# Gate and up projections of a two-layer decoder: one plain step instead of two, ten of eleven steps by seven products

## The reference

```python
def swiglu(h, w_gate, w_up, w_down):
    return (jax.nn.silu(h @ w_gate) * (h @ w_up)) @ w_down

for i in range(DEPTH):                      # DEPTH = 2
    ...                                     # token mixer of layer i
    h = rmsnorm(x, g[2])
    x = x + rmsnorm(swiglu(h, ffn_w_gate[i], ffn_w_up[i], ffn_w_down[i]), g[3])
```

## Time and profile before

| | |
|---|---|
| median of three runs | 1316.03 us (1315.64 to 1317.51) |
| the profiled execution | 1315.58 us |
| its span in the trace | 1313.8 us |
| TensorE busy | 1303.6 us, 99% of the span |
| VectorE busy | 992.3 us, 76% |
| ScalarE busy | 603.2 us, 46% |
| granted TensorE clock, mean | 1.00 of full speed (2.4 GHz) |
| DMA, mean | 110 GB/s |

### The profile page before, as it was taken

One profiled execution on the slowest core, in us unless ns is written; L12 is line 12 of the kernel. 1 busy time (PEld: TensorE's weight loads), 2 busy tenths in 40 slices (PEclk: granted clock), 3 DMA queues, 4 the chain that ended last, 5 costly groups with the idle time before them and its releaser, 6 DMA issues. The chain is left out here.

```text
span 1313.8 us, 19204 instructions
## 1 busy us (share of the span) xinstructions
PE 1303.6 (99%) x7897; PEld 1158.9 (88%) x7897; DVE 992.3 (76%) x1041; ACT 603.2 (46%) x741; POOL 70.1 (5%) x113
## 2 busy tenths in 40 slices
PE   9999999999999999999999999999999999999998
PEld 5888888888889999999888999888898999998886
DVE  7997777789668788887587576577478888874893
ACT  7453444346443444444263455557345344442551
POOL 1000000000010000000000121022010000000000
PEclk9999999999999999999999999999999999999999
DMA  7262515245434333324503132314233233317001
GB/s 257 70 227 65 168 33 162 71 160 186 167 97 129 97 113 93 105 76 159 194 0 113 33 113 72 104 48 161 65 119 106 82 112 97 113 49 272 33 32 64
DMA packets 103414, 145.10 MB, mean 110 GB/s; under 512 B 3581, under 2 KB 77565, under 8 KB 102823
## 3 DMA queue, kind: packets, MB, share of 16 engines
q1 hardware_dynamic: 93168, 136.65, 31.5%
q10 hardware_dynamic: 10166, 7.32, 1.8%
HBM read 137.65 MB, written 8.41 MB: 111 GB/s over the span
## 5 line engine op out<-in xcount | busy, mean ns | idle before, releaser
L2422 PE MATMUL ps<-h_hi,w_hi 128*128 128x256 f32 (+1 forms) x688 | 224.8, 327 | 0.0
L2424 PE MATMUL ps<-h_hi,w_lo 128*128 128x256 f32 (+1 forms) x688 | 223.7, 325 | 0.0
L2423 PE MATMUL ps<-h_lo,w_hi 128*128 128x256 f32 (+1 forms) x688 | 223.6, 325 | 0.0
L1555 DVE TENSOR_TENSOR w_lo<-raw,w_hi 128x2048 fp32r<-128x2048 f32 (+2 forms) x62 | 120.9, 1952 | 72.2 <-ACT w_hi L951 43.3
L2422 PE MATMUL ps<-w_hi,act_hi 128*128 128x512 f32 x432 | 168.7, 391 | 0.1
L2424 PE MATMUL ps<-w_hi,act_lo 128*128 128x512 f32 x432 | 168.2, 389 | 0.0
L2423 PE MATMUL ps<-w_lo,act_hi 128*128 128x512 f32 x432 | 168.1, 389 | 0.0
L2422 PEld LDWEIGHTS ps<-h_hi,w_hi 128*128 128x128 f32 x688 | 130.9, 190 | 10.7
L2424 PEld LDWEIGHTS ps<-h_hi,w_lo 128*128 128x128 f32 x688 | 130.9, 190 | 10.7
L2423 PEld LDWEIGHTS ps<-h_lo,w_hi 128*128 128x128 f32 x688 | 130.9, 190 | 10.4
L1168 ACT ACTIVATE w_hi<-w_sum 128x1024 fp32r<-128x1024 f32 x48 | 50.9, 1061 | 122.0 <-DVE w_sum L1897 122.0
(11 more groups left out here) (333 smaller groups left out, 3233.4 us busy)
## 6 DMA issues: line engine op xcount, KB each, us to landing
raw<-in_ffn_w_down SPq DMA_DIRECT2D x14, 1024.0 KB, 5.7
x<-in_ret_w_in SPq DMA_DIRECT2D x13, 1024.0 KB, 5.2
raw<-in_ffn_w_up SPq DMA_DIRECT2D x24, 512.0 KB, 4.4
raw<-in_ffn_w_gate SPq DMA_DIRECT2D x24, 512.0 KB, 3.9
raw<-in_ret_w_in SPq DMA_DIRECT2D x10, 1024.0 KB, 5.3
down_raw<-in_ffn_w_down SPq DMA_DIRECT2D x8, 1024.0 KB, 10.2
raw<-in_diff_w_in SPq DMA_DIRECT2D x8, 1024.0 KB, 5.4
tmp<-in_ffn_w_gate SPq DMA_DIRECT2D x12, 512.0 KB, 3.9
```

The source lines that it names most:

```text
L1555: nc.vector.tensor_tensor(out_ap, whole, high.bitcast(F32), ALU.subtract).then_inc(done, 1)
L2422: nc.tensor.matmul(out_ap, a_hi, b_hi, start=start, stop=False, skip_group_check=shared)
L2423: nc.tensor.matmul(out_ap, a_hi, b_lo, start=False, stop=False, skip_group_check=shared)
L2424: return nc.tensor.matmul(out_ap, a_lo, b_hi, start=False, stop=stop, skip_group_check=shared)
```

## The change

PLAIN goes from 2 to 1: step 1 of each layer is now done by seven products, and the two calls of `columns`, with their two `prep` on ScalarE and VectorE and the second plain silu and hidden, go away. VectorE and ScalarE get an order of their own for the first step by seven. The sums T1 and T2 of that step are made in `boundary`, ahead of the last two `pre_low`, and its four pieces are loaded into the places (`raw`) where the two plain units were loaded. The places of all later pieces shift by two. TensorE's own code loses the two lines and is otherwise the same. Left out of the diff below: the places' semaphore counts in the down projection.

```diff
@@ -53,7 +53,7 @@
 RETO_N = RET_HEADS * RET_DV // (2 * P) - 4
 FFN_N = FT // 2
 DOWN_N = FFN_N - 4
-PLAIN = 2
+PLAIN = 1
 GU_U = [RETO_U + RETO_N, 0]
 DN_U = [GU_U[0] + 2 * PLAIN, 0]
 DIFF_U = DN_U[0] + DOWN_N
@@ -86,13 +86,14 @@
 PRODUCTS = ("B11", "T2", "T1", "T3", "B21", "B22", "T4")
 LEFT = {"B11": "A11", "T2": "S2", "T1": "S1", "T3": "S3", "B21": "A12", "B22": "S4", "T4": "A22"}
 USED = Order((n, f) for n in SEVEN for f in PRODUCTS)
-SUMS = Order((n, f) for n in SEVEN for f in ("T1", "T2", "T4", "T3"))
-HIGHS = Order([(PLAIN, f) for f in ("T4", "B21", "B22", "B11", "T2", "T1", "T3")]
+SUMS = Order([(PLAIN, f) for f in ("T1", "T2", "T3", "T4")] + [(n, f) for n in SEVEN[1:] for f in ("T1", "T2", "T4", "T3")])
+HIGHS = Order([(PLAIN, f) for f in ("B11", "T2", "T1", "T3", "B21", "B22", "T4")]
               + [(n, f) for n in SEVEN[1:] for f in ("B11", "T1", "T2", "T3", "B21", "B22", "T4")])
-LOWS = Order([(PLAIN, f) for f in ("T4", "B21", "B22", "B11", "T2", "T1", "T3")]
+LOWS = Order([(PLAIN, f) for f in ("B11", "T2", "T1", "T3", "B21", "B22", "T4")]
              + [(n, f) for n in SEVEN[1:] for f in ("B11", "T2", "T1", "T3", "B21", "B22", "T4")])
-S_SUMS = Order((0, f) for f in ("A21", "A22", "A11", "S1", "A12", "S2", "S3", "S4"))
-S_PARTS = Order((0, f) for f in ("S1", "S2", "S4", "S3"))
+S_SUMS = Order((0, f) for f in ("A21", "A22", "S1", "A11", "S2", "A12", "S4", "S3"))
+S_PARTS = Order((0, f) for f in ("S2", "S1", "S3", "S4"))
+PIECE_LOADS = (7, 7, 8, 8, 7, 7)
 
 
 DOWN = ("B11", "T1", "T2", "B21", "T3", "B22", "T4")
...
@@ -455,25 +456,25 @@
 
         def piece(l, n, f):
 
-            at = (4 * (n - PLAIN) + BLOCKS.index(f)) % 6
+            at = (4 * (n - PLAIN) + BLOCKS.index(f) + 2) % 6
             if at < 2:
                 return flat_tmp[:, at * HALF:(at + 1) * HALF]
             slot = (GU_U[l] + at // 2 - 1) % 2
             return raw[slot][:, at % 2 * HALF:(at % 2 + 1) * HALF]
 
         def piece_sem(n, f):
-            return piece_in[(4 * (n - PLAIN) + BLOCKS.index(f)) % 6]
+            return piece_in[(4 * (n - PLAIN) + BLOCKS.index(f) + 2) % 6]
 
         def piece_count(l, n, f):
-            p = 4 * (n - PLAIN) + BLOCKS.index(f)
-            return 16 * ((7 if p % 6 < 4 else 6) * l + p // 6 + 1)
+            p = 4 * (n - PLAIN) + BLOCKS.index(f) + 2
+            return 16 * (PIECE_LOADS[p % 6] * l + p // 6 + (p % 6 > 1))
 
         def form_sum(l, n, f):
 
             if f == "T4":
                 return t4_sum
             if n == PLAIN:
-                return early({"T1": 0, "T2": 1, "T3": 2}[f])
+                return early({"T1": 5, "T2": 6, "T3": 7}[f])
             slot, half = {"T2": (0, 1), "T1": (1, 0), "T3": (1, 1)}[f]
             return w_sum[(GU_U[l] + slot) % 2][:, half * HALF:(half + 1) * HALF]
 
@@ -791,11 +792,11 @@
 
             def load_piece(l, n, f):
                 p = 4 * (n - PLAIN) + BLOCKS.index(f)
-                if p < 2:
+                if p < 4:
+                    sp.wait_ge(w_split, GU_U[l] + p // 2 + 1 + PRIME)
+                elif p < 6:
                     sp.wait_ge(pre_turned, ST * (2 * l + 2))
                     sp.wait_ge(x_added, ST * (2 * l + 1))
-                elif p < 6:
-                    sp.wait_ge(w_split, GU_U[l] + p // 2 + 2 + PRIME)
                 else:
                     m, old = PLAIN + (p - 6) // 4, BLOCKS[(p - 6) % 4]
                     sp.wait_ge(t_made, SUMS.at(l, m, {"B11": "T1", "B12": "T3", "B22": "T3", "B21": "T4"}[old]))
...
@@ -1157,7 +1158,7 @@
                 if n > PLAIN:
                     act.wait_ge(form_used, USED.at(l, n - 1, f))
                 else:
-                    done = {"B11": 3, "T2": 3, "T1": 4, "T3": 4, "B21": 2, "B22": 2, "T4": 0}[f]
+                    done = {"B11": 0, "T2": 0, "T1": 1, "T3": 1, "B21": 2, "B22": 2, "T4": 0}[f]
                     act.wait_ge(w_used, GU_U[l] + done + PRIME)
                 if f[0] == "B":
                     act.wait_ge(piece_sem(n, f), piece_count(l, n, f))
@@ -1199,17 +1200,13 @@
                 nc.scalar.activation(u2, u2, ACT.Silu).then_inc(sil2_made, 1)
 
             def gate_up(l):
-                u = GU_U[l]
-                first, second = u % 2, (u + 1) % 2
-                prep(u + 2, first, used=u)
-                for f in ("S1", "S2", "S4"):
-                    left_high(l, f)
-                prep(u + 3, second, used=u + 1)
+                first = GU_U[l] % 2
+                form_high(l, PLAIN, "B11")
+                left_high(l, "S2")
+                form_high(l, PLAIN, "T2")
+                left_high(l, "S1")
+                form_high(l, PLAIN, "T1")
                 plain_silu(l, 0)
-                for f in ("T4", "B21", "B22", "B11", "T2"):
-                    form_high(l, PLAIN, f)
-                plain_silu(l, 1)
-                form_high(l, PLAIN, "T1")
                 left_high(l, "S3")
                 form_high(l, PLAIN, "T3")
                 for n in SEVEN:
@@ -1217,6 +1214,11 @@
                     if n > PLAIN:
                         second_silu(l, n - 1)
                     copy_p1(l, n)
+                    if n == PLAIN:
+                        form_high(l, n, "B21")
+                        left_high(l, "S4")
+                        form_high(l, n, "B22")
+                        form_high(l, n, "T4")
                     if more:
                         form_high(l, n + 1, "B11")
                     if n > PLAIN:
@@ -1647,6 +1649,9 @@
                 post_add(c, 3)
                 pre_scale(c + 1, 2)
                 pre_scale(c + 1, 3)
+                if c % 2 == 0:
+                    weight_sum(c // 2, PLAIN, "T1")
+                    weight_sum(c // 2, PLAIN, "T2")
                 pre_low(c + 1, 2)
                 pre_low(c + 1, 3)
 
...
@@ -1942,40 +1947,54 @@
 
             def gate_up(l):
                 u = GU_U[l]
-                prep(u + 2, u % 2)
                 dve.wait_ge(w_used, u + PRIME)
                 dve.wait_ge(h_split, ST * (2 * l + 2))
                 whole_left("A21")
                 whole_left("A22")
+                left_add(l, "S1", "A21", "A22", ALU.add)
                 whole_left("A11")
-                left_add(l, "S1", "A21", "A22", ALU.add)
+                left_add(l, "S2", "S1", "A11", ALU.subtract)
                 whole_left("A12")
-                left_add(l, "S2", "S1", "A11", ALU.subtract)
+                left_add(l, "S4", "A12", "S2", ALU.subtract)
+                form_low(l, PLAIN, "B11")
+                left_low(l, "S2")
+                form_low(l, PLAIN, "T2")
+                left_low(l, "S1")
+                form_low(l, PLAIN, "T1")
                 left_add(l, "S3", "A11", "A21", ALU.subtract)
-                left_add(l, "S4", "A12", "S2", ALU.subtract)
-                for f in ("S1", "S2", "S4"):
-                    left_low(l, f)
-                prep(u + 3, (u + 1) % 2)
-                for f in ("T1", "T2", "T4", "T3"):
-                    weight_sum(l, PLAIN, f)
-                plain_hidden(l, 0)
-                for f in ("T4", "B21", "B22", "B11", "T2", "T1"):
-                    form_low(l, PLAIN, f)
+                weight_sum(l, PLAIN, "T3")
                 left_low(l, "S3")
                 form_low(l, PLAIN, "T3")
-                plain_hidden(l, 1)
+                plain_hidden(l, 0)
                 for n in SEVEN:
                     more = n < FFN_N - 1
-                    if n > PLAIN:
-                        make_c21(l, n - 1)
+                    if n == PLAIN:
+                        make_u2(l, n)
                         form_low(l, n, "B21")
-                        second_hidden(l, n - 1)
+                        left_low(l, "S4")
+                        make_u4(l, n)
                         form_low(l, n, "B22")
+                        weight_sum(l, n, "T4")
+                        form_low(l, n, "T4")
+                        make_c22(l, n)
+                        form_low(l, n + 1, "B11")
+                        for f in ("T1", "T2", "T4"):
+                            weight_sum(l, n + 1, f)
+                        form_low(l, n + 1, "T2")
+                        form_low(l, n + 1, "T1")
+                        weight_sum(l, n + 1, "T3")
+                        make_c12(l, n)
+                        form_low(l, n + 1, "T3")
+                        first_hidden(l, n)
+                        continue
+                    make_c21(l, n - 1)
+                    form_low(l, n, "B21")
+                    second_hidden(l, n - 1)
+                    form_low(l, n, "B22")
                     if more:
                         form_low(l, n + 1, "B11")
                     make_u2(l, n)
-                    if n > PLAIN:
-                        form_low(l, n, "T4")
+                    form_low(l, n, "T4")
                     if more:
                         weight_sum(l, n + 1, "T1")
                     make_u4(l, n)
@@ -2613,8 +2632,6 @@
 
             def gate_up(l):
```

(6 more changed lines are left out.)

## The result

The changed kernel takes 1320.05 us (median of 9 runs, 1318.53 to 1321.11); before takes 1316.03 (9 runs, 1315.29 to 1317.51). The ratio is 1.0025, 95% interval 1.0016 to 1.0034: 4.0 us slower. What was forecast as no change is a small loss.

A forecast was written before the change was run, and what follows sets the result against it. TensorE, busy 99%, bounds the kernel, with VectorE feeding it. Per layer 1.64 us saved against 2.8 of stalls leaves 1.14 later: 1315.58 + 2 x 1.14 = 1317.9, on the median 1318.3, range 1315.8 to 1320.4.

The forecast's parts named there:

- TensorE's gain, 1.64 a layer: Step by seven replacing the plain step in each layer: 20.15 us instead of 21.79, 1.64 less, 3.27 in all.
- VectorE's replay: VectorE's new order followed by instruction from 404.67: u4 of step 2 late, TensorE waits 2.2 us before B22.
- The net 1.14 a layer: T4's product of step 2 starts at 456.55 instead of 455.41: each layer 1.14 us later, not 1.64 earlier.
- The boundary sums hidden, 2.5 a layer without cover: Sums T1 and T2, 2.54 us, fit a 2.81 us pause before h's last remainders; otherwise up to 2.5 a layer.
- The clock: Rival, chance 0.05: the 2.2 us stall before B22 of step 2 lowers TensorE's clock, 2 us more a layer, 1322.3.
- The test named for it: Sign: the forecast is wrong if TensorE's granted clock drops in the window 450 to 460.
- The rival of the longer stall: Rival, chance 0.16: stall before B22 of step 2, then step 3, longer by 1 us a layer, 1320.3.
- The gain stays: Rival, chance 0.11 in whole or part: u4 of step 2 ready before 451.0; 1312.8, half the gain 1314.5.

The follow-up runs named there:

- unstalled version: Changed kernel with T4's sum of step 1 made earlier and u2, u4, c22 of step 2 put ahead of less urgent work: 1313.07 us, ratio 0.9977.
- the edit with the halves: Kernel before, with the second plain step's products issued as 192 matmuls of 256 columns instead of 96 of 512: 1319.57 us, ratio 1.0023.
- work in slack: Changed kernel with u2 computed twice more in step 6, where VectorE has idle time: 1320.48 us, ratio 1.0034.
- the repeated run: The changed kernel itself measured once more, unedited, with another profiled execution: 1320.87 us, ratio 1.0034.

## Why the prediction was right, and where it fell short

- *TensorE's gain, 1.64 a layer:* right. The unstalled version gains 3.08 of 3.27, and the edit with the halves shows where it comes from and why it isn't an eighth.
- *VectorE's replay:* right, and this was the term that was to decide. u4 of step 2 to 0.1 us, the pause before B22 2.16 for 2.2, the small stall before T4 of step 1 0.1 for 0.1, before T2 of step 2 0.2 for 0.3, none in step 3. T4's product of step 2 was forecast 456.55 - 416.35 = 40.20 after the start of step 1; layer 1 has it 1033.77 - 993.72 = 40.05 after.
- *The net 1.14 a layer:* 1.0 at this product and 1.1 at that of step 3 (in the layer without a fall, 477.14 - 416.82 against 475.57 - 416.35 before). Twice 1.1 gives 1318.2 on the median of before: the forecast of 1318.3.
- *The boundary sums hidden, 2.5 a layer without cover:* right, though the most it could cost, 2.5, was not reached: undone, the kernel is 3.8 us slower, 1.9 a layer.
- *The clock: the step that failed.* The prediction gave it as a rival with a chance of 0.05 and a price of 2 us a layer, reasoned from a pause of 0.47 that changed nothing, while its own sum made a pause four times as long. It happens in one layer of two, in each of four profiled executions with a pause of 1.88 (two of the changed kernel, one each of the runs with work in slack and with the boundary sums undone), and costs 1.30 where it does: a smaller price, and more often, than the rival had it. 1318.2 + 1.3 = 1319.5; up to 1320.05 half a us remains, see below. Without the fall the change would be inside the bound of 0.2%, with it it is outside. The test named for it, the granted clock between 450 and 460, shows it in this profile, but in two of the four the fall is in layer 1, near 1030, where the test would not have looked.
- *The range:* the time lies inside it partly by luck. It was drawn for errors of the replay and left the clock out; the replay was good to a few tenths, and what carried the time to 0.35 us from the upper end was the clock.
- *The rival of the longer stall:* its number, 1320.3, is nearer to the result than mine, its mechanism did not occur: no hand-over was dearer, and the pause was not longer than 2.2. Only the profile tells the two apart.
- *"The gain stays"* would have needed 2.4 us less chain. That is what the version with u2, u4 and c22 ahead did, and it came to 1313.97.

*The last 0.5 us.* Between the two profiled executions nothing is left over: the last matmul starts 4.27 us later (1312.06 for 1307.79), of which 0.81 is there at the start of step 1 in layer 0, 2.38 comes in that layer up to T4's product of step 3 (1.08 of chain, 1.30 of the fall), and 1.08 in layer 1. The 0.81 is the start of the program, with its own fall of the clock. It is no constant of the changed program: the version with T4's sum early does the same up to there, and its T4 product of step 1 starts at 433.61, for 434.44. How many of the other executions start late, no run shows; half a us of the medians is also inside the interval of the ratio (1.2 us either way).

What stays open is why one layer falls and not the other: the pause alone does not decide it, since both layers have the same.

The Trainium skill ("TensorE: Matmul & The Clock Gate", "What's actually happening") says that the clock is throttled by default and that activity releases it. The fall behind a pause and the return while TensorE is busy agree with that. Why the same pause brings a fall in one layer and none in the other, no run here shows.

## What to carry to other kernels

Where one engine is busy 99% of the time and another one feeds it, forecast a change by replaying the feeder's queue instruction by instruction, with its start-to-start times and its own waits: here that was good to 0.1 us, and it also says which edit repairs the loss (put first what the bound engine wants first, and start a sum that passes through another engine early enough). A forecast pause of TensorE is not paid by its length alone: above the longest pause that the trace shows without harm, add the price of a clock fall as a real term and not as a remote case. And before a difference of 1 us is given to an edit, compare the starts of the two profiled executions: here the first 16 us alone differ by up to 2.0.

## What the runs showed of the hardware

- Pauses of TensorE of 1.0 and 1.67 us, between dense 256-column matmuls, were followed by no fall of the clock in two layers each; 1.88 by one in one layer of two, in each of four profiled executions; 2.40 in one of two; 3.34 in both. In the changed kernel's profile the fall came 1.4 us after the restart, in that of the repeated run 0.5 us after it; both lasted some 3.4 us, in which 256-column matmuls stood 0.21 apart instead of 0.12. Each fall cost 1.26 to 1.31 us.
- In the sparser work at the program's start the length of a pause decides even less: 0.71 us was followed by a fall in the changed kernel's profile, 1.21 (the repeated run) and 1.12 (work in slack) by none. The first rise to 2.4 GHz comes late in some executions: 512-column matmuls are 0.23 apart from 5.54 in before's and still 0.42 apart at 12.3 in that of the halves, 2.0 us of time.
- A sum of 1024 elements that goes through ScalarE delays the remainder behind it to 2.40 us from the sum's start, where 1.14 is its own step: about 1.2 of idle VectorE if nothing stands between.
- Three matmuls of 256 columns cost 0.36, one and a half of 512 columns 0.34: with 256 columns the weight loads are busy throughout (23.03 of 23.03 us), and splitting the columns costs 5.7% of a stage. That the loads set the distance fits this but was not tried by itself.
